# Sample compression of a decoder step: page fills placed among eighths of a sample's products, and the last values stored before the next stage's large load

## What is computed

```
ch = rows.reshape(B, n_ch, CMP_STRIDE, NSA_G, 2, HD)
blk = jnp.concatenate([ch[:, :-1], ch[:, 1:]], axis=2) + cmp_pe[:, None]
flat = blk.transpose(0, 1, 3, 4, 2, 5).reshape(B, n_cmp, NSA_G, 2, CMP_BLOCK * HD)
h = jax.nn.gelu(jnp.einsum('bngcf,cfh->bngch', flat, cmp_w1) + cmp_b1)
out = jnp.einsum('bngch,chd->bngcd', h, cmp_w2)
return rmsnorm(out[..., 0, :], k_norm_cmp), out[..., 1, :], end_pos
```

## Time and profile before

| | before |
|---|---|
| median of 3 executions | 2583.96 us |
| lowest, highest | 2579.82, 2584.76 us |
| the profiled execution's own time | 2569.68 us |
| its span | 2568.1 us |
| mean granted PE clock in it | 0.965 |
| PE busy | 2389.3 us (93%) |
| DVE busy | 1216.1 us (47%) |
| ACT busy | 813.6 us (32%) |
| POOL busy | 321.0 us (13%) |

### The profile page before, as it was taken

The page is one execution under the profiler, slowest core; times in us unless marked ns, Lnnn a source line. Parts: engine busy times, 40 slices in busy tenths (PEclk is TensorE's granted clock), DMA queues, the critical chain, the costliest instruction groups (busy, mean ns, idle before and its releaser), DMA issues. The chain is left out here.

```text
span 2568.1 us, 40403 instructions
## 1 busy us (share of the span) xinstructions
PE 2389.3 (93%) x15386; PEld 2177.1 (85%) x15386; DVE 1216.1 (47%) x2160; ACT 813.6 (32%) x1779; POOL 321.0 (13%) x570
## 2 busy tenths in 40 slices
PE   6988897999877999878799999999999999999999
PEld 6977787999766889744499999987999999999997
DVE  4457665313757777466532323334434333333334
ACT  5354454444435665323321112221311111111110
POOL 1014221012204322355100000000000000000000
PEclk9998699999999999889899999999999999999999
DMA  5012432321110000277301112130211111111111
GB/s 154 21 34 67 137 109 80 98 99 34 43 35 1 1 1 1 56 183 179 98 25 50 50 42 78 50 116 1 83 50 49 34 50 50 50 39 44 50 33 66
DMA packets 216412, 156.77 MB, mean 61 GB/s; under 512 B 76338, under 2 KB 197349, under 8 KB 216164
## 3 DMA queue, kind: packets, MB, share of 16 engines
q1 hardware_dynamic: 186708, 121.96, 16.8%
q0 software_dynamic: 8160, 19.08, 2.8%
q10 hardware_dynamic: 21360, 13.22, 1.7%
HBM read 142.76 MB, written 15.59 MB: 62 GB/s over the span
## 5 line engine op out<-in xcount | busy, mean ns | idle before, releaser
L177 PE MATMUL ps<-brT_r,ff_wih 128*128 128x344 f32 x1008 | 322.0, 319 | 0.0
L179 PE MATMUL ps<-brT_r,ff_wi_r 128*128 128x344 f32 x1008 | 321.6, 319 | 0.0
L178 PE MATMUL ps<-xnT_r,ff_wih 128*128 128x344 f32 x1008 | 321.3, 319 | 0.0
L3765 ACT ACTIVATE ff_sa<-ps 128x344 f32<-128x344 f32 x66 | 30.3, 459 | 563.5 <-PE ps L179 563.5
L177 PE MATMUL ps<-x_r,mg_wh 128*128 128x344 f32 x576 | 185.4, 322 | 6.5 <-DVE xnT_r L165 6.5
L177 PEld LDWEIGHTS ps<-brT_r,ff_wih 128*128 128x128 f32 x1008 | 189.6, 188 | 1.0
L179 PEld LDWEIGHTS ps<-brT_r,ff_wi_r 128*128 128x128 f32 x1008 | 189.4, 188 | 0.0
L178 PEld LDWEIGHTS ps<-xnT_r,ff_wih 128*128 128x128 f32 x1008 | 189.0, 187 | 0.4
L178 PE MATMUL ps<-xnT_r,mg_wh 128*128 128x344 f32 x576 | 184.7, 321 | 0.0
L3801 DVE TENSOR_TENSOR x<-x,ps 128x512 f32<-128x512 f32 (+1 forms) x198 | 134.8, 685 | 100.9 <-PE ps L179 100.2
L179 PE MATMUL ps<-x_r,mg_w_r 128*128 128x344 f32 x552 | 176.2, 319 | 0.0
(11 more groups left out here) (618 smaller groups left out, 5871.5 us busy)
## 6 DMA issues: line engine op xcount, KB each, us to landing
ff_wi<-in_w_ffn_in SPq DMA_DIRECT2D x42, 512.0 KB, 5.2
mg_w<-in_w_in SPq DMA_DIRECT2D x23, 512.0 KB, 4.2
ff_wo<-in_w_ffn_out SPq DMA_DIRECT2D x11, 1024.0 KB, 4.9
s_pages<-in_cache_kv_slc POOLq DMA_DIRECT2D x128, 64.0 KB, 2.8
s_pages<-in_cache_kv_slc SPq DMA_DIRECT2D x128, 64.0 KB, 2.8
sc_X<-in_cache_kv_cmp SPq DMA_DIRECT2D x56, 128.0 KB
sc_X<-in_cache_kv_cmp POOLq DMA_DIRECT2D x56, 128.0 KB, 2.4
mg_w<-in_w_branch SPq DMA_DIRECT2D x23, 256.0 KB, 4.6
```

Source lines behind the costliest of these rows:

```text
L177: nc.tensor.matmul(out, wh, xh, start=(first and k == 0), stop=False)
L178: nc.tensor.matmul(out, wh, xl, start=False, stop=False)
L179: ins = nc.tensor.matmul(out, wl, xh, start=False, stop=(last and k == n - 1))
L3765: nc.scalar.activation(sa[:, s % 2, :], ps[:, s % 2, 0:BLK], ACT.Silu).then_inc(silued, 1)
```

## The change

Three things change, all in `stage_s_compress`.

First, PE's order. A quarter is cut into two eighths of 12 matmuls. In the turn of sample b, the four fills of sample b+1 stand before eighths 0, 1, 3 and 4 (instead of before eighths 0, 2, 4 and 6). `project(b-1)` stands behind eighth 3, which is where it stood. The waits of a quarter pass to its first eighth. Second, ACT's gelu of the keys' sums and DVE's copy of the projection go behind the split of the sample's fourth fill instead of the third. Third, SP stores the last values before it issues the 1 MB load.

```
-                sp.wait_ge(hid, 2 * B)
-                sp.dma_start(tok_weights(M, 1, "raw"), tok_group(M, 1)).then_inc(M["tok_in1"], 16)
                 sp.wait_ge(okept, B)
                 sp.dma_start(M["vc_kept"][:, VE:], vc[:, :, :, :].rearrange("p b g d -> p (b g d)")[:, VE:]
                              ).then_inc(stored, 16)
+                sp.wait_ge(hid, 2 * B)
+                sp.dma_start(tok_weights(M, 1, "raw"), tok_group(M, 1)).then_inc(M["tok_in1"], 16)
                 sp.wait_ge(kdone, 4)
...
-                def quarter(b, k):
-                    cc = k // 2
-                    if k == 0:
+                def eighth(b, k, part_):
+                    cc, lo = k // 2, k % 2 * 8 + 4 * part_
+                    if k == 0 and part_ == 0:
                         pe.wait_ge(x_low, NF * (b + 1))
-                    if k % 2 == 0 and b >= 1:
+                    if lo == 0 and b >= 1:
                         pe.wait_ge(activated, 2 * (b - 1) + cc + 1)
...
-                                    for r in range(k % 2 * 8, k % 2 * 8 + 8)], first=(k % 2 == 0), last=(k % 2 == 1))
-                    if k % 2:
+                                    for r in range(lo, lo + 4)], first=(lo == 0), last=(lo == 12))
+                    if lo == 12:
                         ins.then_inc(hid, 1)
...
-                    for k in range(4):
-                        if b + 1 < B:
-                            fill((b + 1) * NF + k)
-                        quarter(b, k)
-                        if k == 1 and b >= 1:
+                    for e in range(8):
+                        if b + 1 < B and e in (0, 1, 3, 4):
+                            fill((b + 1) * NF + (0, 1, 3, 4).index(e))
+                        eighth(b, e // 2, e % 2)
+                        if e == 3 and b >= 1:
                             project(b - 1)
...
-                        if k == 2:
+                        if k == 3:
                             gelu(b, 0)
...
-                        if k == 2 and b >= 1:
+                        if k == 3 and b >= 1:
                             out(b - 1)
```

More of the change, by code:

```diff
@@ L2559, in fill @@
                     ins.then_inc(turned, 1)
-                def quarter(b, k):
-                    cc = k // 2
-                    if k == 0:
+                def eighth(b, k, part_):
+                    cc, lo = k // 2, k % 2 * 8 + 4 * part_
+                    if k == 0 and part_ == 0:
                         pe.wait_ge(x_low, NF * (b + 1))
-                    if k % 2 == 0 and b >= 1:
+                    if lo == 0 and b >= 1:
                         pe.wait_ge(activated, 2 * (b - 1) + cc + 1)
-                    if k % 2 == 0 and b == 0:
+                    if lo == 0 and b == 0:
                         pe.wait_ge(w_low, cc + 1)
```

## The result

The changed kernel took 2562.71 us as median of five executions (2557.95 to 2572.21). The kernel before took 2579.82 as median of five beside them (2574.49 to 2584.76); the three that the prediction started from, with the median 2583.96, are among them. The ratio is 0.9937 with a 95% interval of 0.9908 to 0.9965, that is 16 us faster, between 9 and 24. The gain of 13.4 us that was forecast would be a ratio of 0.9948, which the interval holds.

The account below looks back on a forecast made before the run. PE was taken to bound the stage, waiting for DVE's splits. Stage: 13.4 + 1.5 - 1.9 - 0.45 = 12.5 us; with 0.9 at SP's end, 13.4 off 2583.96 gives 2570.6 us, range 2565.5 to 2577.0.

Parts of the forecast that it names:

- What bounds the stage: PE sets the stage's time; it waits seven times, 11.9 us in all, for DVE's split before a first product.
- The gain of the removed waits: PE's seven waits of first products go, since 48 products and a fill follow the fourth fill: 13.4 us gained.
- the new waits: PE's third fill waits 0.32 us in samples 1 to 6, 1.9 in all; the first sample's fourth fill waits 0.45.
- The clock: Sample 1's half-speed stretch on PE, behind a 1.83 us wait, goes: 1.5 us gained.
- The slower rival: Many short PE stops each bring a half-speed stretch costing 1.5 us; with 14, 2591.6 us; chance 0.02.
- The moved gelu, the pages: ACT's moved gelu and DVE's copy cost nothing, and page loads need 15.2 us of 22 available, so no wait.
- SP's end: SP no longer waits 2.6 us for the last values; the last keys' store binds ACT next, leaving 0.9 us gained.
- The step that failed: Final step for the whole kernel: the 13.4 us gain, taken from the three-execution median 2583.96, gives 2570.6 us.

Follow-up runs that it names:

- fills_late: The changed kernel with its four fills ahead of eighths 1, 3, 5 and 7 instead of 0, 1, 3 and 4; median 2606.09 us, ratio 1.0117.
- sp_only: The kernel before with only the last values' store moved ahead of the 1 MB load; median 2576.42 us, ratio 0.9999.
- load_last: The changed kernel with the 1 MB load moved behind the store of the last keys as well; median 2564.67 us, ratio 0.9957.

## Why the prediction was right, and why its number was wrong

- **What bounds the stage.** Right. The seven waits of first products went, and `fills_late` brought them back in the length worked out from the same durations (27.1 against 28).
- **The gain of the removed waits and the new waits.** The forecast was 12.5 us for the stage; the first profiles have 140.85 - 128.55 = 12.3, the means of two and of three profiles 140.9 - 128.9 = 12.0. The new waits show as 0.2 us of idle time, seven of them, for the 0.32 and 0.45 forecast, and the periods are those that were worked out (16.3).
- **The clock.** Right for sample 1, which has 1.00 after in every profile of the change. But the forecast tied the fall to the length of the wait, "its longest wait between two samples that both have fills", and passed over the 2.39 us of the last sample, which left the clock at 1.00. The seven waits of 3.9 us in `fills_late` were each followed by a fall; the five of 1.5 us never were; between them length alone does not decide. And the clock does fall in sample 0's turn, behind the wait for pages, for longer in five of nine profiles, which the forecast did not count. The slower rival, short waits of PE that throttle it, needed a fall of the clock behind the 0.2 us waits. There was none: the samples from 1 on had 1.00. The rule of the Trainium skill (TensorE: Matmul & The Clock Gate, A second HAM failure mode: psum-queue depth-cycling), which would have brought it about, is not borne out for waits this short and 13 to 16 us apart.
- **The moved gelu, the pages.** Right: no cost, no wait for pages after the first.
- **SP's end.** 0.9 us was forecast; the first pair of profiles has 12.68 - 12.09 = 0.6, `sp_only` 0.8. The mechanism was as told, with the last keys' store next in line. Two things were missed. The removed wait varies (2.2, 2.6 and 4.3 us in three profiles), so against the mean of two profiles of the kernel before (13.5) and of three of the change (11.8) the end brings 1.7. And I took 3.5 us for that store as the row had it, without saying what it costs alone: 2.4 to 2.7 us where nothing large is ahead of it. What the Trainium skill says of the order of completions (DMA: Bandwidth & Descriptors, Queues, rings and completion order) fits `load_last`, with 2.7 us against 3.5 to 3.9, and the ten profiles with the load ahead, in which the store never landed before it.
- **The step that failed** is the last one: "I assume the same difference for the median: 2583.96 - 13.4". The gain was right and the number it was taken from was not. Three executions had a median of 2583.96; five sets of 5 to 23 had 2575.85 to 2579.82. Taken from 2579.82, the forecast would have been 2566.4. And the range gave the run-to-run spread 2 or 3 us, while the samples' attention alone moves by 9 us with its clock (181.6 to 190.8), so that a median of five can be 3 us off on either side. The first five executions of the change were low (2562.71), later sets had 2564.37 and 2567.71; the first ones of the kernel before were high. Both errors lay on the same side. The forecast of 13.4 us stands against 12.6 ± 2 over all executions and 13.7 by the ruler. That it fits the ruler so closely is in part luck: on the means the stage brought 0.5 us less than forecast and the end 0.8 more.

The 14.3 us between the profiled execution (2569.68) and the median of 2583.96 stood in the prediction and were themselves a sign of this spread, but no width was drawn from them. What decides which clock the samples' attention gets in an execution was not looked for, and stays open.

## What to carry to other kernels

- For work that is split between engines, write down when the last piece is ready after its start (here 6.4 us) and count the work that the waiting engine has in between; put the last piece early and leave the long run of products behind it. What then waits are the pieces that stand too close, and a short independent task, such as the projection, fits in that gap.
- A wait is dearer than its idle time where the clock falls behind it: 3.9 us of idle time were followed by a stretch at half speed that cost 1.7 or 3.0 us more, every time; 1.5 us of idle time were not. In between it went both ways (1.83 us with a fall, 2.39 without), so look at the clock behind each wait.
- Give small stores that someone waits for their place ahead of a large load on the same queue; they land earlier, though here the microsecond won did not show in the median. And before a gain of half a per cent is put on a median, look how far the stages that nobody touched differ between two profiles of one program.

## What the runs showed that I had not expected

The time of the samples' attention follows its granted clock: 181.6 us at 0.95 and 190.3 to 190.8 at 0.89, with one program giving 184.8 in one execution and 190.7 in another. This one stage carries more of the scatter than everything behind it (1300.6 to 1302.3 us).

A 128 KB store behind a 1 MB load took 7.1, 7.6 and 9.2 us in three executions, 4.8 to 4.9 ahead of it with the load issued next, and 4.1 with the load issued last.
